# A hybrid decoder step on one core: the experts' up matrices ordered by ACT, gate and down by SP

## What is computed

```python
def expert_block(args):
    xb, e = args
    return (jax.nn.silu(xb @ w_exp_gate[e]) * (xb @ w_exp_up[e])) @ w_exp_down[e]
...
out = jnp.zeros((T, D_MODEL), F32).at[tok_s].add(ybuf[dest].astype(F32) * w_s[:, None])
```

## Time and profile before

| | us |
|---|---|
| median of 3 runs | 1644.14 (1641.23 to 1644.26) |
| the profiled execution, its own time | 1645.93 |
| its span, first to last instruction | 1644.3 |
| stage `experts`, first weight order to last scatter order | 1098.6 to 1613.3 |
| `combine` behind it | to 1644.3 |

### The profile page before, as it was taken

One profiled execution on the slowest core, in us unless ns is written; L12 is line 12 of the kernel. 1 busy time (PEld: TensorE's weight loads), 2 busy tenths in 40 slices (PEclk: granted clock), 3 DMA queues, 4 the chain that ended last, 5 costly groups with the idle time before them and its releaser, 6 DMA issues. The chain is left out here.

```text
span 1644.3 us, 26410 instructions
## 1 busy us (share of the span) xinstructions
PE 1279.5 (78%) x10642; PEld 798.6 (49%) x10642; DVE 510.9 (31%) x1011; ACT 266.5 (16%) x540; POOL 186.4 (11%) x247
## 2 busy tenths in 40 slices
PE   5999959989994586688334899929878878887881
PEld 4875545779993454445223785523333323333330
DVE  2002364845646352654332211251111101110113
ACT  2000232401220122443000001201111101110110
POOL 0000250200000430111311000001101111111000
PEclk9999977899998697799666999959989989998996
DMA  7021121151001853332534661159999999999974
GB/s 302 16 81 63 46 68 59 67 132 18 5 4 57 245 180 108 99 102 104 163 122 177 223 273 64 42 192 336 406 406 405 414 405 411 407 413 406 415 296 169
DMA packets 85482, 324.84 MB, mean 198 GB/s; under 512 B 25249, under 2 KB 53074, under 8 KB 70682
## 3 DMA queue, kind: packets, MB, share of 16 engines
q1 hardware_dynamic: 69578, 293.86, 46.9%
q0 software_dynamic: 11184, 25.17, 4.7%
q10 hardware_dynamic: 4608, 4.20, 0.8%
HBM read 306.32 MB, written 28.92 MB: 204 GB/s over the span
## 5 line engine op out<-in xcount | busy, mean ns | idle before, releaser
L2465 DVE TENSOR_TENSOR e_g<-e_g,PS 64x512 f32<-64x512 f32 x32 | 22.1, 690 | 333.1 <-ACT e_g L2432 333.1
L281 PE MATMUL PS<-scr,p_w 128*128 128x272 f32 (+2 forms) x448 | 105.7, 399 | 6.1 <-DVE scr L348 6.1
L884 PE MATMUL PS<-scr 128*128 128x272 f32 x384 | 92.2, 404 | 21.1 <-DMA scr<-in_w_gates 21.1
L2378 PE MATMUL PS<-first,e_xs 128*64 128x512 f32 x352 | 88.2, 659 | 22.8 <-DMA first<-in_w_exp_up 22.1
L2378 PE MATMUL PS<-second,e_xs 128*64 128x512 f32 x352 | 86.8, 650 | 24.5 <-DMA second<-in_w_exp_up 23.8
L2378 PE MATMUL PS<-e_w,e_xs 128*64 128x512 f32 x320 | 80.3, 660 | 23.5 <-DMA e_w<-in_w_exp_up 23.5
L281 PEld LDWEIGHTS PS<-scr,p_w 128*128 128x128 f32 (+2 forms) x448 | 84.0, 188 | 27.4 <-issue 6.9
L884 PEld LDWEIGHTS PS<-scr 128*128 128x128 f32 x384 | 75.1, 196 | 37.7 <-DMA scr<-in_w_gates 21.8
L2036 PE MATMUL PS<-m_oT,xe 128*128 128x272 f32 x256 | 64.7, 413 | 22.4 <-DMA m_oT<-scratch_ob_dram 17.8
L2321 POOL DMA_INDIRECT xe<-scratch_h_dram,toks x32 | 30.5, 954 | 387.7 <-PE PS L2368 276.8
L293 PE MATMUL PS<-p_w,scr 128*128 128x512 f32 (+1 forms) x192 | 70.7, 529 | 0.0
(11 more groups left out here) (535 smaller groups left out, 2038.7 us busy)
## 6 DMA issues: line engine op xcount, KB each, us to landing
first<-in_w_exp_gate SPq DMA_DIRECT2D x11, 2048.0 KB, 18.0
first<-in_w_exp_up SPq DMA_DIRECT2D x11, 2048.0 KB, 22.4
first<-in_w_exp_down SPq DMA_DIRECT2D x11, 2048.0 KB, 23.3
second<-in_w_exp_gate SPq DMA_DIRECT2D x11, 2048.0 KB, 27.3
second<-in_w_exp_up SPq DMA_DIRECT2D x11, 2048.0 KB, 31.7
second<-in_w_exp_down SPq DMA_DIRECT2D x11, 2048.0 KB, 22.9
e_w<-in_w_exp_gate SPq DMA_DIRECT2D x10, 2048.0 KB, 27.5
e_w<-in_w_exp_up SPq DMA_DIRECT2D x10, 2048.0 KB
```

Source lines behind the costliest of these rows:

```text
L281: last = nc.tensor.matmul(out[:, n], w[:, s % NW, c, a:a + m], hT[:, c, n * TH:n * TH + TH], start=(c == 0), stop=(c == KC - 1))
L884: last = M(gate_ps(u)[:, n], wgate[:, u % 2, c, :], hT[:, c, n * TH:n * TH + TH], start=(c == 0), stop=(c == KC - 1))
L2378: last = M(ps, xs[:, b, c, :], w[s][m][:, c * DE:c * DE + DE], start=(c == 0), stop=(c == KC - 1))
L2465: V.tensor_tensor(g[:, b, :], g[:, b, :], psU, ALU.mult).then_inc(h_out, 1)
```

## The change

The loop of SP skips the up matrix (m == 1) for all experts from n = 3 on. In its place ACT orders the load of up n + 3 directly behind its silu of expert n: the call `load_up`, 29 of them (up 3 to up 31). The silu waits until both halves of `gate_up(n)` are through, which is the same condition that SP waited for. Gate and down stay with SP, with their waits. The overflow code is not changed.

```diff
--- before.py
+++ after.py
@@ -2302,6 +2302,8 @@
             def _(sp):
                 for n in range(2, NE):
                     for m in range(3):
+                        if n >= NS and m == 1:
+                            continue
                         if n >= NS:
                             sp.wait_ge(gu_mm if m < 2 else y_mm, 2 * (n - NS + 1))
                         sp.dma_start(w[n % NS][m][:], expert_matrix(io, m, n)).then_inc(w_in[n % NS][m], 16)
@@ -2431,17 +2433,23 @@
                     act.wait_ge(gu_mm, 2 * n + 2)
                     A(g[:, b, :], psG, ACT.Silu).then_inc(silu_out, 1)
 
+                def load_up(n):
+                    act.dma_start(w[n % NS][1][:], expert_matrix(io, 1, n)).then_inc(w_in[n % NS][1], 16)
+
                 def y_high(n, b):
                     act.wait_ge(y_mm, 2 * n + 2)
                     A(ye[:, b, DE:D], psY[1], ACT.Copy).then_inc(y_out, 1)
 
                 rows_out(0, 0)
                 silu(0, 0)
+                load_up(NS)
                 rows_out(1, 1)
                 for n in range(NE):
                     b = n % 2
                     if n + 1 < NE:
                         silu(n + 1, 1 - b)
+                    if n + 1 + NS < NE:
+                        load_up(n + 1 + NS)
                     if n + 2 < NE:
                         rows_out(n + 2, b)
                     if n >= 2:
```

## The result

The changed kernel takes 1647.41 us at the median of 20 runs, the kernel before 1642.56 us at the median of 20 runs beside it: ratio 1.0024, 95% interval 1.0014 to 1.0034. The change makes the kernel slower by 0.24%, some 4 us (2.3 to 5.6). The forecast was +1.0 us, with a range from -4 to +9.

The account below looks back on a forecast made before the run. The prediction took the arrival of weights to bound the expert stage. ACT's orders 0, head -2.0, middle 0 and PE late at the end gave +1.0 us in all, a median of 1645.1 us, range 1641.5 to 1648.

Parts of the forecast that it names:

- What bounds the kernel: Expert stage: it runs at the rate at which weights arrive, 408 GB/s, 16.26 us per expert; PE itself needs 12.42.
- ACT's orders: Behind each silu: 29 orders of 0.36 us at the median fit in a 0.88 us gap; cost 0.
- The head: From 1132 to 1136 us: up 4, ordered about 5 us earlier, fills the dry queue gap; -2.0 us.
- The order of arrival: Mid-stage: ups on their own queue land some 10 us after their order, and PE waits for gates instead.
- The end: Last experts: late loads come closer than PE can take them, PE is the bound for two turns; +1.0 us taken.
- slow clock: Last turns: PE's clock has fallen while it waited, so a turn takes 14.2 us; gate_up(31) starts +2.1 us.
- quick clock: Last turns: PE's clock stays up, turns take 12.42 us; gate_up(31) starts +0.3 us.
- The middle: Mid-stage: same bytes, engines never dry, the period stays at 16.26 us; 0, if two queues run like one.
- The slower rival: Weight stream: turns between two weight queues cost time, up to 1.05 us per expert, a quarter expected, 1652 us; chance 0.20.
- The sum: Whole kernel: profiled execution 1645.93 + 1.0 = 1646.9 us; for the median 1644.14 + 1.0 = 1645.1 us.
- The faster rival: Weight stream: mixing two queues loses less, 27 x 0.3 = -8 us, 1636 us; chance 0.15.
- pieces are served in order of ordering: Both queues: ups would land as before, only the head's gap is gained, -2.0 us, 1642.1 us; chance 0.10.

Follow-up runs that it names:

- e5: Kernel before with only the first piece of the inner dimension multiplied in gate_up and down, all loads by SP: 1630.48 us, -0.85% against before.
- e3: Kernel before, but only the ups of experts 3 and 4 ordered by ACT: -0.10% against before (-0.24 to +0.03).
- e8: The changed kernel run and traced once more, nothing altered: stream 500.6 us, start of gate_up(31) 499.4 us after gate 2's order.
- e2: Kernel before, but only ups 29, 30 and 31 ordered by ACT: +0.23% against before (+0.07 to +0.39).
- e1: Changed kernel, but ups 29 to 31 ordered by SP again: +0.15% against before (-0.01 to +0.30).
- second pair: The changed kernel and the kernel before, each traced once more unaltered: 405 and 409 GB/s from 1160 to 1560 us.
- e11: Kernel before with only the first inner piece multiplied; ACT orders ups and the downs of odd experts: 1638.11 us, -0.42% against before.
- e6: Changed kernel, ups by ACT, with only the first inner piece multiplied in gate_up and down: 1634.82 us, -0.48% against before.
- e10: Kernel before with only the first inner piece multiplied, every load from expert 3 on ordered by ACT: 1632.17 us, -0.73% against before.

## Why the prediction was right, and where it was off

- **What bounds the kernel**, the arrival of weights: right. Full shares in the middle of all traces, and seven eighths fewer matmuls in gate_up (e5) bring only 14 us. In the traces some 9 us of them lie behind the start of gate_up(31), where no weight but down 31 is still to come, and 3.2 us before it.
- **ACT's orders, 0**: right. 0.34 us each, during the silu; the copy behind it starts no later.
- **The head, -2.0 us**: right. The gap is gone in the changed trace, and e3 alone has -1.8 us of stream and -2.0 us of start.
- **The order of arrival**: right. Gates are waited for, ups land early, though after 15 us and not 10.
- **The end, PE as the bound**: right in mechanism, and nearly so in size. The forecast put gate_up(31) 3.0 us behind gate 31 (a start of +1.0 where gate 31 lands at -2.0). The two traces have 3.0 and 3.6 us. PE was without a wait for two turns in e8, as forecast, and for three in the first trace: there the waits had become more uneven (9.0 us for gate 28, then none), so gate 28 set the end. Counted from gate 2's order, expert 29 started 9.0 and 7.4 us later than before, not 5. e8 shows the forecast's case of the slow clock: 14.1 and 12.4 us from expert 29 to expert 31, where the text has 14.2 and 12.42, worth +2.1 us; expert 29 started 1.8 us later than that sum assumed (472.8 us after gate 2's order, not 471.0), which makes the measured 3.9. The forecast had taken +1.0, midway to the quick clock, so 1.1 us of the miss are this choice. e2 shows that the last ups alone are enough for the measured loss (+0.23%), and e1 that PE's lateness goes away with the last three ups on SP.
- **The middle, 0**: the term that was mis-sized. Two weight queues cost rate, 405 against 408 GB/s (405 against 409 in the second pair). A rate other than 408 GB/s was one of the prediction's own signs that it would be wrong. e3 and e1 both fill the head's gap and end with ups on SP; between them the stream grows by 2.6 us with 24 more ups on ACT's queue. With small matmuls the cost is 3.6 us. The slower rival had this as its mechanism, with a bound of 1.05 us per expert and a quarter of it, 0.26, as its guess; it is about 0.1 us (2.6 us over the 24 ups), below the 3.3 us from which it was to decide. Its way of counting, so much for each turn between two queues, does not stand: e11 has more turns and the same stream.
- **The sum**: the start can be taken apart into the stream and PE's distance from its end. Head -1.8; two queues +2.2, which is not measured by itself but is what the stream's +0.35 leaves once the head is taken off, with whatever the short queues at the end cost; PE late at the end +3.5 (4.95 against 1.45 us between the start of gate_up(31) and the landing of down 31, means of two traces each). That is +3.9 us of start by construction, and 4.0 were timed. The forecast had -2.0, 0 and +3.0. What made +1 into +4 is, for the most part, the term set to zero for lack of a row with two full queues.
- **The faster rival** (two queues lose less) fell: e6 and e11 are slower than e5 and e10. That pieces are served in order of ordering fell with the ups that land after 15 us. The Trainium skill's rule for kernel authors ("DMA: Bandwidth & Descriptors") that spreading DMAs over several engines doesn't help for bandwidth holds, and the runs add that here it costs: 406 against 410 GB/s. The prediction had concluded from the rule that neither rival would occur; for the slower one this conclusion does not stand.
- The outcome of +0.24% is just past the bound of 0.2%: it is the forecast's mechanism together with a small part of the slower rival's, while the text had taken the two for alternatives. The direction was right and the size was off, +4 us for +1. That the median of 1647.41 us lies within the forecast's own range (1641.5 to 1648) is partly luck: the kernel before came out at 1642.56 us, not at the 1644.14 on which the range was built, and 0.24% on top of the latter is 1648.1.

## What to carry to other kernels

In this stage, bound by the arrival of its weights, an order that was given earlier brought bytes earlier only where the queues were dry (2 us at the head). Everywhere else it only changed which bytes came first, and ACT's lightly filled queue acted as a priority: 15 us to landing against 34. Give priority to what the engine needs soonest, and read the last turns of the stage separately: there every byte that came too early has pushed one back that is needed now, and PE, which takes 12.4 us for a turn at its fastest, could not catch up. Here the gain lay in the opposite move, one queue with downs behind the next gates and ups (-0.38%).

## What the runs showed of the hardware

- Two weight queues that are both full ran 0.5 to 1% slower than one, 406 and 407 against 410 and 409 GB/s with small matmuls and 405 against 408 with the full ones, and as slow with shares of 64 to 32% as with 48 to 48%. One queue is as fast on ACT as on SP (409 and 410 GB/s).
- A gather on POOL's queue lands after 8.6 to 8.8 us beside one full weight queue and after 11.7 to 12.6 us beside two.
- The DMA engines ended far apart: in the kernel before the DMA share falls from 1586 us on, while the last matrix lands at 1598.9. A landing is that of the last part, and the mean rate does not show how far behind the slowest engine is.
